# Two transformer blocks in one kernel: buffers allocated in another order, input tiles 512 and 256 columns apart

## What is computed

```python
# first block, layer l: 14 projections and 4 gates, four mixers, a gated merge
hx = modulate(rmsnorm(x, norm_w[l]), shift_x, scale_x)      # and hc of the context
px = split_proj(hx @ w_in[l])                               # 1024 -> 11008
pc = split_proj(hc @ w_in[l])                               # layer 1: ret_k, ret_v, att_k, att_v only
merged = sum(sigmoid(g) * (br @ w_branch[l, i]) for i, (g, br) in enumerate(...))
x = x + gate_x * (merged @ w_out[l])
# second block: an RG-LRU mixer in layer 0, gated linear attention in layer 1, and after each
u = causal_dwconv(h @ ffn_w_up[i])                          # 1024 -> 5632
x = x + gt_f * rmsnorm_2((gelu(g) * val) @ ffn_w_down[i])   # 2816 -> 1024
```

## Time and profile before

| | |
|---|---|
| median of 3 runs | 1750.58 us (1748.8 to 1752.02) |
| span of the profiled execution | 1751.7 us, 28134 instructions |
| TensorE busy | 1709.8 us (98%), 10612 matmuls |
| VectorE busy | 1394.4 us (80%) |
| ScalarE busy | 883.4 us (50%) |
| HBM | 298.45 MB read, 171 GB/s over the span |

### The profile page before, as it was taken

How to read it: one execution, slowest core, us unless ns; L and a number is a source line. 1 busy time by engine, 2 the same in 40 slices (tenths; PEclk the granted TensorE clock), 3 DMA queues, 4 the chain that set the end, 5 groups by cost and what they waited for, 6 DMA issues and landing times.

```text
span 1751.7 us, 28134 instructions
## 1 busy us (share of the span) xinstructions
PE 1709.8 (98%) x10612; PEld 1492.3 (85%) x10612; DVE 1394.4 (80%) x2532; ACT 883.4 (50%) x1530; POOL 0.2 (0%) x4
## 2 busy tenths in 40 slices
PE   7999999999999999999999999999999999999998
PEld 4788887777888888897888999998899888889997
DVE  7699996546789998888777699878888667778874
ACT  5322324456332233353346754567766657576563
POOL 0000000000000000000000000000000000000000
PEclk8999999999999999999999999999999999999999
DMA  9583211211766776744333388844555545346553
GB/s 339 210 293 115 87 59 48 97 37 37 248 231 241 274 255 216 240 145 144 116 102 97 95 280 311 267 136 158 187 189 181 182 153 166 113 140 208 183 189 111
DMA packets 224774, 301.32 MB, mean 172 GB/s; under 512 B 6000, under 2 KB 188656, under 8 KB 224256
## 3 DMA queue, kind: packets, MB, share of 16 engines
q1 hardware_dynamic: 224640, 299.52, 51.2%
HBM read 298.45 MB, written 1.05 MB: 171 GB/s over the span
## 4 chain that ended last, share of the span: by engine, by line
PE 48%; DVE 3%; ACT 3%; issue 2%; DMA 0%; DVEq 0%; ACTq 0%
PE bank L700 10%; PE bank L695 10%; PE bank L697 10%; PE bank L1081 3%; PE bank L1082 3%; PE bank L1083 3%; ACT w_hi L1397 1%; PE bank L671 1%; PE bank L672 1%; PE bank L673 1%; PE bank L1148 1%; PE bank L1211 1%; DVE w_lo L2178 1%; PE bank L926 0%; PE bank L1061 0%
## 5 line engine op out<-in xcount | busy, mean ns | idle before, releaser
L2178 DVE TENSOR_TENSOR w_lo<-ring,w_hi 128x1024 fp32r<-128x1024 f32 (+1 forms) x432 | 490.8, 1143 | 182.8 <-ACT w_hi L1397 179.8
L1397 ACT ACTIVATE w_hi<-ring 128x1024 fp32r<-128x1024 f32 (+1 forms) x432 | 425.5, 991 | 171.4 <-PE bank L700 92.6
L695 PE MATMUL bank<-h_hi,w_hi 128*128 128x256 f32 (+2 forms) x2086 | 378.1, 323 | 1.3 <-ACT w_hi L1397 1.0
L700 PE MATMUL bank<-h_hi,w_lo 128*128 128x256 f32 (+2 forms) x2086 | 371.1, 320 | 0.1
L697 PE MATMUL bank<-h_lo,w_hi 128*128 128x256 f32 (+2 forms) x2086 | 371.0, 320 | 0.0
L695 PEld LDWEIGHTS bank<-h_hi,w_hi 128*128 128x128 f32 x2086 | 309.0, 188 | 36.1 <-ACT w_hi L1397 2.9
L700 PEld LDWEIGHTS bank<-h_hi,w_lo 128*128 128x128 f32 x2086 | 309.8, 188 | 29.9 <-DVE w_lo L2178 0.3
L697 PEld LDWEIGHTS bank<-h_lo,w_hi 128*128 128x128 f32 x2086 | 309.8, 188 | 29.8
L1384 ACT ACTIVATE work<-bank 128x512 f32<-128x512 f32 (+1 forms) x134 | 67.3, 521 | 254.7 <-PE bank L700 173.0
L1384 ACT ACTIVATE arena<-bank 128x256 f32<-128x256 f32 (+4 forms) x119 | 55.2, 468 | 205.8 <-PE bank L700 122.9
L2479 DVE SCALAR_TENSOR_TENSOR arena<-arena,params 128x512 f32<-128x512 f32 (+1 forms) x240 | 130.7, 618 | 0.0
(11 more groups left out here) (320 smaller groups left out, 2138.6 us busy)
## 6 DMA issues: line engine op xcount, KB each, us to landing
ring<-in_w_in SPq DMA_DIRECT2D x86, 1024.0 KB, 5.5
arena<-in_ada_w_t SPq DMA_DIRECT2D x96, 512.0 KB, 6.0
ring<-in_ffn_w_up SPq DMA_DIRECT2D x44, 1024.0 KB, 5.1
ring<-in_ffn_w_down SPq DMA_DIRECT2D x20, 1024.0 KB, 5.1
ring<-in_w_branch SPq DMA_DIRECT2D x32, 512.0 KB, 4.7
arena<-in_w_mod_t SPq DMA_DIRECT2D x32, 512.0 KB, 5.2
ring<-in_gla_w_in SPq DMA_DIRECT2D x12, 1024.0 KB, 5.3
ring<-in_w_out SPq DMA_DIRECT2D x8, 1024.0 KB, 6.1
```

The costliest lines, as they stand in the source:

```text
L695: pe.matmul(out[:, 0:n], w[0][:, k, :], hi(k, n), start=k == 0, stop=False)
L700: m = pe.matmul(out[:, 0:n], w[1][:, k, :], hi(k, n), start=False, stop=k == tiles - 1)
L1397: nc.scalar.activation(hi, src, ACT.Copy)\
L2178: step(nc.vector.tensor_tensor(lo, src, hi.bitcast(F32), ALU.subtract), f"lo {u}", *(["used " + stream[w_units[u][0]][0]] if w_units[u][3] ...
```

## The change

The order of the allocations changes, and with it where buffers lie; the views of `h_hi` and `h_lo` change their strides. No instruction is added or taken away.

- `tables` goes from before `xT` to behind `w_lo`, followed by `warm`; `mods` (336 columns) goes to between `h_lo` and `w_hi`. `h_hi` and `h_lo` keep their 8 x 528 columns.
- the view of layer 1 is the same as that of layer 0 (512 columns, 512 apart, from column 0), so the gap of 16 columns is gone from it;
- `x` is 256 columns, 256 apart (before: 272 apart). `g` stays 272 apart, `y` stays where it was, `x1` in the arena stays 258 apart.

```diff
+BESIDE = 16
+N_MODS = 2 * 48 + 2 * 16 + 2 * 48 + 2 * 32 + 24 + 24
...
-        params, tables = sbuf("params", N_PARAM), sbuf("tables", N_TABLE)
+        params = sbuf("params", N_PARAM)
         xT = sbuf("xT", KT * 2 * S)[:].rearrange("p (t s) -> p t s", t=KT)
 
-        h_parts = [sbuf(n, KT * (2 * S + 16), F32R)[:].rearrange("p (t s) -> p t s", t=KT) for n in ("h_hi", "h_lo")]
-        h_hi, h_lo = (h[:, :, 16:16 + 2 * S] for h in h_parts)
-        h_flat = [h.rearrange("p t s -> p (t s)") for h in h_parts]
-        in_tiles = [h[:, 0:KT * (S + 16)].rearrange("p (t s) -> p t s", t=KT) for h in h_flat]
-        g_hi, g_lo = (h[:, :, 0:LATE_N] for h in in_tiles)
-        x_hi, x_lo = (h[:, :, 0:S] for h in in_tiles)
-        y_hi, y_lo = (h[:, KT * (S + 16):KT * (2 * S + 16)].rearrange("p (t s) -> p t s", t=KT) for h in h_flat)
-        both_hi, both_lo = (h.rearrange("p t s -> p (t s)")[:, 0:KT * 2 * S].rearrange("p (t s) -> p t s", t=KT)
-                            for h in h_parts)
+        h_flat = [sbuf(n, KT * (2 * S + BESIDE), F32R)[:] for n in ("h_hi", "h_lo")]
+
+        def tiles_at(at, n, each):
+
+            return [h[:, at:at + KT * each].rearrange("p (t s) -> p t s", t=KT)[:, :, 0:n] for h in h_flat]
+
+        h_hi, h_lo = both_hi, both_lo = tiles_at(0, 2 * S, 2 * S)
+        g_hi, g_lo = tiles_at(0, LATE_N, S + BESIDE)
+        x_hi, x_lo = tiles_at(0, S, S)
+        y_hi, y_lo = tiles_at(KT * (S + BESIDE), S, S)
         in_hi, in_lo = (both_hi, h_hi, x_hi), (both_lo, h_lo, x_lo)
 
+        mods = sbuf("mods", N_MODS)
         w_parts = [sbuf(n, PARTS * KT * P, F32R)[:].rearrange("p (u t n) -> p u t n", u=PARTS, t=KT) for n in ("w_hi", "w_lo")]
...
+        tables, warm = sbuf("tables", N_TABLE), sbuf("warm", 8)
...
-        warm = sbuf("warm", 8)
-        mods = sbuf("mods", 2 * 48 + 2 * 16 + 2 * 48 + 2 * 32 + 24 + 24)
```

## The result

The changed kernel takes 1755.03 us (median of 8 runs, 1754.11 to 1757.14), the kernel before 1751.39 beside it: a ratio of 1.0025 (95% interval 1.0016 to 1.0033). It is 0.25% slower, where 1732 was forecast. The profiled execution has a span of 1753.2 us.

What follows compares the result with a forecast made beforehand. TensorE was taken as the bound, with only its product spacing able to change. Gains of 16.1 + 3.4 + 2.0 us less 2.9 of waits made 18.6 off the 1750.58 us median: 1732, range 1708 to 1768.

Steps and rivals of the forecast that it cites:

- What bounds the kernel: Whole kernel: TensorE is what ACT and VectorE wait for, so only the spacing of its products can change.
- Where they lie: Matmul operands: spacing depends on D, weight start minus input start, modulo 128 columns; 227.2 against 232.3 ns by addresses.
- 256-wide at D = 80: 256-wide products on h: spacing falls from 117.4 to 113.3 ns, 3936 products, 16.1 us gained.
- The arena's 256-wide: 256-wide products on arena tiles: spacing falls from 120 to 113.3 ns, 504 products, 3.4 us gained.
- 512-wide at constant non-zero D: 512-wide products, about 3000 moving off D = 0: spacing taken as 227 ns, no change, no cost.
- C: Rival: 512-wide products settle at 232.3 ns when D is nonzero, costing 15.3 us; chance 0.27, or 0.08 cancelled by 256-wide gain.
- The 384 of layer 1 and x: Layer 1's 240 context-tile and 144 x-tile 512-wide products: 232.3 to 227.2 ns, 2.0 us gained.
- Layer 1's merge giving half back: Layer 1's merge, VectorE and DMA nearly full: half of about 5.8 us gained returns as waits, 2.9 us.
- addresses do nothing: Rival: addresses have no effect and layer 1 is slow for another reason; 1750.6 us, chance 0.05.

Runs made afterwards that it cites:

- e4: Kernel before, with the three input views tightly spaced and all beginning at column 64, so D = 64 for every input tile; 1757.62 us, ratio 1.0036.
- e8: Changed kernel with layer 0's view of h beginning 16 columns on, its 512-wide products at D = 64 instead of 80; 1743.56 us.
- e1: Kernel before, same allocation and layer 0 at D = 0, with only the 256-wide views of layer 1 and x moved to D = 80; 1737.67 us, ratio 0.9918.
- e5: e1 plus the 258-column view g spaced 320 apart from column 48, a constant D of 16 modulo 64; 1739.91 us, ratio 0.9931.
- e7: e5 plus the high parts of layer 1's branches beginning at column 48, putting 256 arena products at D = 16 modulo 64; 1738.38 us, ratio 0.9928.
- e3: Kernel before, same allocation, with the changed kernel's views, every input tile at D = 0; 1757.85 us, ratio 1.0035.

## Why the prediction was wrong

**What bounds the kernel** held: TensorE stays at 97 to 98%, and every run's time followed the sum of its spacings, to within some 4 us. The clock was not at full speed all the time behind the first slice, though the earlier trace rows has a 9 in each: a slice is 43.8 us long, and its digit hides short falls. In the trace of before it was granted at 0.50 from 799.40 to 802.80 us, where 512-wide products stand 427 ns apart and not 232; TensorE had waited 1.95 us just before, at the start of layer 1. The traces of e4 and e8 have no such fall at that place. These steps are among those left out of the means.

**Where they lie** held as a cause and was wrong in its period: 64 columns, not 128 (e4). That addresses matter at all, the other half of it, was right: kernels with the same instructions, timed over several runs, lie between 1737.67 and 1764.82 us by addresses alone. That D counts and not the input's own place is tested by two places only: by the order of the allocations, the input and the weights of the changed kernel lie 8 columns modulo 64 from those of e1, and at the same D the two agree (114.25 and 113.7; at 512 columns 233.2 and, in layer 1, 233.4).

**256-wide at D = 80**, right in kind: 117.6 to 114.25 where 113.3 was taken, 13.1 of the 16.1 us. The rest is a second steady pace, 117.7: 640 of the 3868 spacings in the changed kernel are 117 or 118 ns, 217 of 3872 in e1. The timeline's line at 985.50 is one such run. Most of them, 481 in the changed kernel, lie in layer 1's merge, where the gates' products on h alternate with branch products on the arena: the gates take 117.6 ns there in the changed kernel and in e8, whose arena stands at 112, and 113.8 in e1 and e5, whose arena stayed at 0. So the products beside a run bear on its pace; how, and what decides it outside the merge, stays open.

**The arena's 256-wide** were mis-sized: 117.85 for 113.3, so 1.1 of the 3.4 us. They stand at 112, and I gave them the value of 80. Modulo 64 these are 48 and 16, two different places, and in e7 their products at 16 gained less than half of what was summed.

**512-wide at constant non-zero D** is the step that failed. "I take 227, no change", about 3000 products at nothing: this was my estimate, and no run shows 227 for a 512-wide product at D = 80 or 112. The runs show 233.2 on h, 229.2 on the arena and 231.2 in the row products, 16.6 us together. Nor do the widths share their good values of D: at 0 and 80, 512 columns take 227.1 and 233.2 ns, 256 columns 119.9 (e3) and 114.25. There was a row that spoke to it, the one C leans on: layer 1's 512-wide products at 232.3. I read it as the price of a changing D, and that reading stands: sorted by tile, the spacings of layer 1 in the trace of before are 230.9 to 232.8 at all eight, the tiles at D = 0 and 64 among them (231.5 and 232.7, 29 products each). The step from there failed, that a constant D takes this price off whatever its value. Constant at 80 the products take 233.2; constant at 0 modulo 64 they take 227.6, with e8's one edit, and in layer 1 itself 227.3 (e3).

**The 384 of layer 1 and x** were to go from 232.3 to 227.2. The 240 of layer 1 went to D = 80 and from 231.9 to 233.2, for the same reason. The 144 on x are row products and went to 48, from 231.6 to 229.3.

**Layer 1's merge giving half back** was not put to the test by the changed kernel, as little gain arrived there: its gates went from 118.3 to 117.6. TensorE's idle time from 1000 to 1145 us is 145.00 - 141.99 = 3.0 us before and 145.00 - 141.81 = 3.2 after:

```profile
1000.00:1145.00 145.00, 141.81 (x1195) 140.92 (x1194) 127.69 (x225) 86.52 (x150) 0.00 (x0) 1.00 0.80 271
```

In e1 the gain did arrive, with the gates at 113.8. From the first to the last start of the arena's 256-wide products the merge lasts 142.9 us before and 141.0 in e1, 1.9 less where the spacings account for 2.7: about a third came back there, and not half.

**The rivals.** The range begins at 1708, where each of 3384 512-wide products saves 7.0 ns. No run shows such a saving: no kind of 512-wide product in the table above has a mean under 226.8 ns in any trace, and the fastest kernel takes 1737.67 us. The outcome is C in the case in which the 256-wide gain all the same, given 1749 and a chance of 0.08; 1755 lies in the range from 1708 to 1768 and outside the forecast's own, 1725 to 1740. C was also right on its deciding point: a 512-wide product lost 6.1 ns on h, less than the 7.4 at which it was to outweigh a full gain, but the gain was not full. The time stood near that of "addresses do nothing" (1750.6), and by the time alone the two are hardly told apart (0.25%, where the prediction counts 0.2% as no change); the groups by shape tell them apart at once.

## What to carry to other kernels

Where matmuls run back to back, compare their start-to-start distance for each streamed width and each operand placement; the same shape at 227 and 233 ns with no wait between was here a matter of where the stationary and the streamed operand lie to each other. Choose the start column of each view by itself, for its own width, from a run at that very width and difference: here it cost no instruction and gave 0.8%, while one common difference for all (0, 64 or 80) cost 0.2 to 0.4%. And where no row shows a shape at the very difference in question, a row of the same shape at another difference (232.3 at 512 columns) counts for more than an estimate with no row behind it.

## What the runs showed of the hardware

- The spacing of these fp32r products, each with its own weights, went with the difference of the two operands' start columns modulo 64 (256 bytes): 227.1 to 234.3 ns at 512 columns, 113.7 to 119.9 at 256. At 64 it was that of 0, 227.1 and 119.9 (e4, e3); at 16 (row products on the arena) that of 80 (on h), 233.2 at 512 columns. Between the two widths at D = 0 lie 107 ns for 256 columns.
- It is not smooth and hung on the exact width: 16 gave 113.7 at 256 columns (80 in e1) and 120.9 at 258 (e5); 12 and 20 gave 119.2 and 119.3 at 256.
- Where D changes from tile to tile, 512-wide products took 230.9 to 232.8 at every tile (layer 1 of before), those at 0 and 64 too (231.5 and 232.7), where a constant 0 gave 227.3 (e3).
- Steady runs settled on one pace or a repeating pattern: 226.7 at D = 0 (512), 120.0 at D = 0 and 113.3 or 117.7 at 16 (256), and 231 and 236 in turn at 16 (512). No run here shows the cause.
